# The first layer's mixer in another order: recurrence beside gate, k and v projections, heads between q tiles, last 16 tokens in blocks of 8 heads

## What is computed

```
proj = u @ w_in                      # gate 1024, xr 1024, q 1024, k 128, v 128 columns
xr = causal_dwconv(xr, conv_w, conv_b)                        # 4 taps
r = sigmoid(xr @ w_a + b_a); i = sigmoid(xr @ w_x + b_x)      # 8 blocks of 128
log_a = -8 * r * softplus(-lam)
h_t = a_t h_(t-1) + sqrt(1 - a_t^2) * i_t * xr_t
y_a = gelu(gate) * h
# 16 query heads of 64, 2 key heads; each token sees the last 128 tokens and the 16 first
s = q k^T / 8 - slope * distance      # masked
p = exp(s - mx) / (sum + exp(sink - mx)), mx = max(row maximum, sink)
y = concat([y_a, p v]) @ w_out
```

## Time and profile before

| | us |
|---|---|
| median of 3 runs | 3022.61 (3022.34 to 3024.46) |
| the profiled execution | 3022.86 |
| its span, first to last instruction | 3020.9 |
| TensorE busy | 2573.4 (85%) |
| VectorE busy | 783.7 (26%) |
| ScalarE busy | 538.1 (18%) |
| mean granted TensorE clock | 0.913 of full |

### The profile page before, as it was taken

One profiled execution on the slowest core, in us unless ns is written; L12 is line 12 of the kernel. 1 busy time (PEld: TensorE's weight loads), 2 busy tenths in 40 slices (PEclk: granted clock), 3 DMA queues, 4 the chain that ended last, 5 costly groups with the idle time before them and its releaser, 6 DMA issues. The chain is left out here.

```text
span 3020.9 us, 36570 instructions
## 1 busy us (share of the span) xinstructions
PE 2573.4 (85%) x15266; PEld 1670.1 (55%) x15266; DVE 783.7 (26%) x1880; ACT 538.1 (18%) x1351; POOL 15.7 (1%) x23
## 2 busy tenths in 40 slices
PE   3999976598998998878777749789899799998998
PEld 1785743387542443323232228547787688666876
DVE  1010156601211111111111122370441225623431
ACT  2110112301111221111111111331111111421110
POOL 0000000000000000000000000000000000100000
PEclk7999996899799999989988979759999899998999
DMA  6132330045369999999999953103233233122432
GB/s 257 70 112 97 112 143 25 6 153 209 149 267 421 420 420 421 420 421 420 421 421 421 421 237 126 56 1 112 98 137 121 104 140 140 56 76 92 140 117 78
DMA packets 88054, 608.36 MB, mean 201 GB/s; under 512 B 10512, under 2 KB 12944, under 8 KB 17200
## 3 DMA queue, kind: packets, MB, share of 16 engines
q1 hardware_dynamic: 84704, 599.82, 50.3%
q10 hardware_dynamic: 3088, 5.78, 0.5%
q0 software_dynamic: 96, 0.39, 0.0%
HBM read 604.91 MB, written 1.05 MB: 201 GB/s over the span
## 5 line engine op out<-in xcount | busy, mean ns | idle before, releaser
L482 PE MATMUL bank<-arena,ring 128*128 128x272 f32 (+2 forms) x3712 | 890.1, 403 | 37.4 <-DVEq L544 18.4
L482 PEld LDWEIGHTS bank<-arena,ring 128*128 128x128 f32 x3712 | 711.2, 192 | 212.2 <-issue 45.4
L2064 PE MATMUL bank<-arena 128*32 128x512 f32 x2304 | 286.0, 618 | 47.6 <-DMA arena<-in_w_e 47.6
L508 PE MATMUL bank<-arena,ring 128*128 128x272 f32 x1216 | 284.9, 398 | 6.6 <-DVE arena L1567 6.1
L508 PEld LDWEIGHTS bank<-arena,ring 128*128 128x128 f32 x1216 | 233.9, 193 | 57.5 <-DVE arena L1567 7.0
L1455 DVE TENSOR_TENSOR arena<-bank,arena 128x256 f32<-128x256 f32 x56 | 23.8, 425 | 844.1 <-PE bank L2043 844.1
L2064 PE MATMUL bank<-ring,arena 128*32 128x512 f32 x1280 | 166.2, 633 | 47.5 <-DMA ring<-in_w_e 47.4
L2064 PEld LDWEIGHTS bank<-arena 128*32 128x32 f32 x2304 | 64.4, 111 | 213.5 <-DMA arena<-in_w_e 105.9
L2081 PE MATMUL bank<-arena 128*32 128x256 f32 x1760 | 115.8, 404 | 44.5 <-DMA arena<-in_w_e 40.5
L1555 DVE SCALAR_TENSOR_TENSOR arena<-arena,par 128x272 f32<-128x272 f32 x296 | 148.6, 502 | 10.5
L2081 PE MATMUL bank<-ring,arena 128*32 128x256 f32 x1824 | 117.7, 406 | 29.4 <-DMA ring<-in_w_e 26.1
(11 more groups left out here) (361 smaller groups left out, 2009.5 us busy)
## 6 DMA issues: line engine op xcount, KB each, us to landing
arena<-in_w_e SPq DMA_DIRECT2D x224, 1024.0 KB, 25.9
ring<-in_w_e SPq DMA_DIRECT2D x160, 1024.0 KB, 26.2
ring<-in_w_up SPq DMA_DIRECT2D x44, 1024.0 KB, 4.8
ring<-in_w_l SPq DMA_DIRECT2D x37, 1024.0 KB, 4.8
ring<-in_w_ada SPq DMA_DIRECT2D x24, 1024.0 KB, 6.3
ring<-in_w_proj SPq DMA_DIRECT2D x24, 1024.0 KB, 4.8
ring<-in_w_down SPq DMA_DIRECT2D x32, 704.0 KB, 4.0
ring<-in_w_merge SPq DMA_DIRECT2D x16, 1024.0 KB, 4.8
```

The source lines that it names most:

```text
L482: mm = pe.matmul(o[:, 0:n], ring[:, s, k * 256 + c * P:k * 256 + (c + 1) * P], rhs(k), start=(k == 0), stop=(k == KT - 1))
L508: mm = pe.matmul(o[:, 0:n], ring[:, s, k * P:(k + 1) * P], rhs(part * kt + k), start=(part == 0 and k == 0), stop=(part == parts - 1 and k ...
L2064: mm = pe.matmul(bank[q * GROUP:(q + 1) * GROUP, 4 + g % 2, :], xe[:, (g // CHUNK) % 2, k, s:s + GROUP], w[:, q * 512:(q + 1) * 512], star ...
```

## The change

The columns of the input weights are laid out in another order: xr, gate, k and v, q.

The recurrence runs beside the projections. PE projects xr (4 units), one gate unit, the recurrence products of tiles 0 to 3, a gate unit, those of tiles 4 to 7, two gate units, then k and v. ACT copies the gate tiles as they are, and between them does sigmoids, tanh, exponentials and the square root. After the root it takes the 8 Gelus from SBUF, and then copies k and v. DVE does all 8 `lru_input`, waits for the root, does all 8 `lru_scan`, and only then begins on the heads.

The heads are worked on between the q tiles. PE does q tile j, the turn of head 2j-2, the values of pair j-2, the scores of head 2j, the turn of 2j-1 and the scores of 2j+1. The scores contract over all 128 rows: k lies in two copies `kz`, each with zeros in the half of the other key head, cleared by POOL. Only tokens 0 to 255 are done per head, in two strips side by side in one bank. Score strips and turned probabilities have four buffers instead of three and two. The banks are 0 to 2 for scores, 3 and 4 for turned probabilities and 5 for values.

The last 16 query tokens of 8 heads are laid side by side, 128 rows (`q_end`). Two such blocks (i = 16 and 17) go through the same steps with 272 columns. Slopes, sinks and penalties are laid out for them. The maximum with the sink and the change of sign are one instruction, with the sinks negated ahead.

Phases 10 and 11 are gone (later ones are renumbered), and the first products of the output projection wait for the single recurrence tiles and for the last pair of heads.

```diff
-    w0 = np.concatenate([w0[:, :2 * D], w0[:, 2 * D:3 * D][:, swap], w0[:, 3 * D:]], axis=1)
+    w0 = np.concatenate([w0[:, D:2 * D], w0[:, :D], w0[:, 3 * D:], w0[:, 2 * D:3 * D][:, swap]], axis=1)
...
# ScalarE
+            def gate_tiles(unit):
+                for n in (2 * unit, 2 * unit + 1):
+                    o, free = tile_out(act, at, n % 2 == 1)
+                    act.activation(ga[:, n, :], o[:, 0:L], ACT.Copy).then_inc(free, 1)
...
+            for unit in range(2):
+                gate_tiles(unit)
+                for n in range(4 * unit, 4 * unit + 4):
+                    lru_sigmoids(n)
             act.wait_ge(sem("lru_gate_read"), 8)
             act.wait_ge(sem("nlru_ready"), 1)
             for n in range(8):
                 act.activation(th[:, n, :], rg[:, n, :], ACT.Tanh, scale=lru2[:, n:n + 1]).then_inc(sem("lru_tanh"), 1)
+            gate_tiles(2)
             act.wait_ge(sem("lru_tanh"), 8)
             for n in range(8):
                 act.activation(rg[:, n, :], rg[:, n, :], ACT.Exp, scale=nlru[:, n:n + 1]).then_inc(sem("lru_decay"), 1)
+            gate_tiles(3)
+            act.wait_ge(sem("lru_ratio"), 8)
+            act.activation(th[:, :, :], th[:, :, :], ACT.Sqrt, scale=2.0).then_inc(sem("lru_root"), 1)
+            act.wait_ge(sem("bank_read0"), at.out // 2)
+            act.wait_ge(sem("bank_read1"), at.out // 2)
+            for n in range(8):
+                act.activation(ga[:, n, :], ga[:, n, :], ACT.Gelu_apprx_tanh).then_inc(sem("lru_gelu"), 1)
+            o, free = tile_out(act, at, False)
+            for s in range(2):
+                ins = act.activation(kz[64 * s:64 * s + 64, s, :], o[64 * s:64 * s + 64, 0:L], ACT.Copy)
+            ins.then_inc(free, 1)
...
+            for j in range(10):
+                if j >= 1:
+                    swa_exp(2 * j - 2)
+                    swa_exp(2 * j - 1)
+                if j < 8:
+                    o, free = tile_out(act, at, j % 2 == 1)
+                    act.activation(q0[:, j, 0:T], o[:, 0:T], ACT.Copy)
+                    act.activation(q_end[:, j, :], o[:, T:L], ACT.Copy).then_inc(free, 1)
+                if j >= 1:
+                    swa_copy(2 * j - 2)
+                if j >= 2:
+                    swa_result(j - 2)
+                if j >= 1:
+                    swa_copy(2 * j - 1)
...
# VectorE
+            for n in range(8):
+                lru_input(n)
+            dve.wait_ge(sem("lru_root"), 1)
+            dve.wait_ge(sem("lru_decay"), 8)
+            for n in range(8):
+                lru_scan(n)
...
+                dve.scalar_tensor_tensor(out=sc[:, b, 0:width], in0=cst("pen", 0 if i < HEADS2 else 3 * P, width),
+                                         scalar=cst("slope", i, 1), in1=bank[:, i % 3, 0:width],
+                                         op0=ALU.mult, op1=ALU.add).then_inc(sem("swa_masked"), 1)
+                dve.wait_ge(sem("swa_masked"), i + 1)
+                for t, (a, z) in enumerate(swa_spans(i)):
+                    ins = dve.reduce_max(smx[:, b, t:t + 1], sc[:, b, a:z], AX_X)
+                chain(ins)
+                n = len(swa_spans(i))
+                dve.tensor_scalar(snm[:, b, 0:n], smx[:, b, 0:n], -HD ** -0.5, nsink[:, i:i + 1], ALU.mult, ALU.min)\
+                   .then_inc(sem("swa_negmax"), 1)
...
+            for n in range(9):
+                swa_mask(2 * n)
+                swa_mask(2 * n + 1)
+                swa_probs(2 * n)
+                swa_probs(2 * n + 1)
...
# TensorE
-            project(pe, at, 12, ub_k, L)
+            project(pe, at, 4, ub_k, L)
+            for half in range(2):
+                project(pe, at, 1, ub_k, L)
+                for n in range(4 * half, 4 * half + 4):
+                    lru_gates(n)
+            project(pe, at, 2, ub_k, L)
...
+            def swa_scores(i):
+                if i >= 3:
+                    pe.wait_ge(sem("swa_masked"), i - 2)
+                b = i % 3
+                if i < HEADS2:
+                    j, s = i // 2, i % 2
+                    pe.wait_ge(sem(f"bank_read{(q_read + j) % NL}"), (q_read + j) // NL + 1)
+                    for t0 in (0, P):
+                        mm = pe.matmul(bank[:, b, t0:t0 + t0 + P], q0[:, j, t0:t0 + P], kz[:, s, 0:t0 + P], start=True, stop=True)
+                else:
+                    mm = pe.matmul(bank[:, b, 0:L], q_end[:, :, :].rearrange("p j t -> p (j t)"), kz[:, i - HEADS2, :], start=True, stop=True)
+                mm.then_inc(sem("swa_scores"), 1)
...
+            for j in range(10):
+                if j < 8:
+                    q_tile(j)
+                if j >= 1:
+                    swa_turn(2 * j - 2)
+                if j >= 2:
+                    swa_values(j - 2)
+                if j < 9:
+                    swa_scores(2 * j)
+                if j >= 1:
+                    swa_turn(2 * j - 1)
+                if j < 9:
+                    swa_scores(2 * j + 1)
+            swa_values(8)
+            project_deep(pe, at, 1, 2 * KT, lambda k: mix[:, k, :], L, first=first_mix)
```

More of the change, by code:

```diff
@@ L1094, in _ @@
[L1094 to L1106, removed]
@@ L1146, in _ @@
             conv_silu(CT - 1)
-            phase(act, 15)
+            phase(act, 13)
             def ssm_square(n):
@@ new lines, in swa_probs @@
+            def swa_probs(i):
+                b, n = i % 4, len(swa_spans(i))
+                dve.wait_ge(sem("swa_exp"), i + 1)
+                chain(dve.tensor_tensor(ssk[:, b, 0:n], ssk[:, b, 0:n], sden[:, b, 0:n], ALU.add))
+                chain(dve.reciprocal(ssk[:, b, 0:n], ssk[:, b, 0:n]))
+                for t, (a, z) in enumerate(swa_spans(i)):
+                    ins = dve.tensor_scalar(sc[:, b, a:z], sc[:, b, a:z], ssk[:, b, t:t + 1], None, ALU.mult)
+                ins.then_inc(sem("swa_probs"), 1)
@@ L1662, in _ @@
             post_norm("l0_post")
-            phase(dve, 12)
+            phase(dve, 10)
             ffn(0)
@@ L1712, in _ @@
                         read_x(i)
[L1713 removed]
+            phase(dve, 13)
             dve.wait_ge(sem("ssm_cb"), 1)
@@ L1768, in _ @@
             post_norm("l1_post")
-            phase(dve, 16)
+            phase(dve, 14)
             ffn(1)
@@ L1773, in _ @@
             post_norm("f1_post")
-            phase(dve, 17)
+            phase(dve, 15)
         @block.gpsimd
@@ L1784, in _ @@
             pool.memset(ys[:, :, :], 0.0).then_inc(sem("ys_cleared"), 1)
-            for n in range(6, 16):
+            for n in range(6, 10):
+                phase(pool, n)
+            pool.memset(kz[64:128, 0, :], 0.0)
+            pool.memset(kz[0:64, 1, :], 0.0).then_inc(sem("kz_cleared"), 1)
+            for n in range(10, 14):
                 phase(pool, n)
@@ L1789, in _ @@
                 pool.tensor_tensor(zs[:, n, :], zs[:, n, :], xb[:, n, :], ALU.mult).then_inc(sem("ssm_gated"), 1)
-            for n in range(16, LAST_PHASE + 1):
+            for n in range(14, LAST_PHASE + 1):
                 phase(pool, n)
@@ L2216, in _ @@
             at.unit += 1
-            pe.wait_ge(sem("lru_loaded"), 16)
-            for n in range(8):
-                pe.wait_ge(sem("xc_ready"), n + 1)
-                if n >= 2:
-                    pe.wait_ge(sem("lru_gate_read"), n - 1)
-                b = 2 * (n % 2)
-                pe.matmul(bank[:, b, 0:L], wlru[:, 0, n, :], xc[:, n, :], start=True, stop=True)
-                pe.matmul(bank[:, b + 1, 0:L], wlru[:, 1, n, :], xc[:, n, :], start=True, stop=True)\
-                  .then_inc(sem("lru_gates"), 1)
@@ new lines, in swa_turn @@
+            def swa_turn(i):
+                pe.wait_ge(sem("swa_probs"), i + 1)
+                if i >= 2:
+                    pe.wait_ge(sem("pt_ready"), i - 1)
+                p = sc[:, i % 4, :]
+                if i < HEADS2:
+                    for c in range(3):
+                        mm = pe.transpose(bank[:, 3 + i % 2, c * P:(c + 1) * P], p[:, c * P:(c + 1) * P], ident)
+                else:
+                    for c, (s0, m) in enumerate(TOK):
+                        mm = pe.transpose(bank[0:m, 3 + i % 2, c * P:(c + 1) * P], p[:, s0:s0 + m], ident)
+                mm.then_inc(sem("swa_turned"), 1)
@@ new lines, in swa_values @@
+            def swa_values(n):
+                pe.wait_ge(sem("pt_ready"), 2 * n + 2)
+                if n >= 1:
+                    pe.wait_ge(sem("swa_result"), n)
+                spans = ((0, T, 0, P), (P, T, T, P)) if n < 8 else ((0, P, 0, P), (0, P, P, P), (0, P, T, META))
+                for c, (a, z, at0, m) in enumerate(spans):
+                    for s in range(2):
+                        mm = pe.matmul(bank[64 * s:64 * s + 64, 5, a:z], v0[0:m, c, 64 * s:64 * s + 64],
+                                       pt[0:m, (2 * n + s) % 4, at0:at0 + z - a],
+                                       start=(c == 0), stop=(c == len(spans) - 1), skip_group_check=True)
+                mm.then_inc(sem("swa_pv"), 1)
@@ L2270, in _ @@
```

(4 more changed lines are left out.)

230 lines of the change are left out of this document (99 added, 131 removed).

## The result

| | before | after | both orders and the tail (last experiment) |
|---|---|---|---|
| median, us | 3023.53 | 2949.87 | 2928.24 |
| lowest to highest, us | 3022.34 to 3026.22 | 2947.8 to 2955.23 | 2925.79 to 2928.47 |
| ratio to before, with 95% interval | | 0.9757 (0.9745 to 0.9768) | 0.9679 (0.9666 to 0.9692) |
| span of the profiled run, us | 3020.9 | 2946.0 | 2925.0 |
| first projection product to first output product, us | 232.0 | 154.45 | (order differs) |

The change is worth 74 us by the medians; 2949.87 was measured and 2948 forecast. I call it the stretch. The row above it I call the mixer.

The account below looks back on a forecast made before the run. The heads' loop through TensorE, VectorE and ScalarE at the low clock was taken as the bound, projections by TensorE elsewhere. Cutting 232.0 us to 156.7 saves 75.3, giving 2948 us, range 2938 to 2972 (its own 2940 to 2962).

Parts of the forecast that it names:

- Projections and recurrence products: Before the heads: reordered tiles and recurrence pairs put TensorE at 54.4 us after two gate units, 78.4 after v.
- The stall at ScalarE's queue: Before the first q tile: TensorE waits 9.1 us for ScalarE's root, Gelus and k copies; bounds 3.6 to 14.
- Table loads: Before the Gelus on ScalarE: 1.3 us taken; the skill's added drain would make the sum 1.4 us larger.
- The rounds: One q tile with a pair of heads' transposes, scores and values: 6.95 us, TensorE longest, at full clock.
- The cover: Within each pair of heads: 4.6 us of TensorE work hides 4.0 us of VectorE and ScalarE, 0.6 to spare.
- The tail: After the last q tile: heads 14 and 15, then the two end blocks, 6.0 and 6.9 us, waits near 3.
- The output projection's clock: At the output projection's start: 0 to 2 us of gain if the clock stays up; 0 taken.
- The sum: First projection product to first output product: 232.0 before, 156.7 after, so 75.3 us saved.
- The rivals: For the whole kernel: low clock 3002 us, chance 0.11; no overlap 3049, 0.04; nothing moves 3015 to 3030, 0.02.
- The low clock: In the heads: TensorE stays at half clock, rounds of 13.9 us, kernel 3002 us; chance 0.11.
- The rounds overlapped as drawn: Against the rival that VectorE and ScalarE work follows the q tile: rounds 20.7 us, kernel 3049 us; chance 0.04.

Follow-up runs that it names:

- both orders and the tail (last experiment): Changed kernel with ScalarE's square root queued last, scans spread over the rounds, and early output-projection products filling TensorE's waits after the last q tile: 2928.24 us, ratio 0.9679.
- values head after head: Changed kernel with a pair's value products issued one head after the other instead of alternating between array halves: ratio 0.9756.
- both orders: Changed kernel with ScalarE's Gelus and k and v copies ahead of the square root, and scans spread over the first seven rounds: 2934.5 us, ratio 0.9701.
- the kernel without interleaving: Changed kernel with all eight q tiles projected before the first head instead of between the heads: ratio 0.9837.

## Why the prediction was right, step by step

*Projections and recurrence products.* Forecast 54.4 and 78.4 us from the first product. In the trace the later gate units start at 54.5 and the v tile ends at 78.4.

*The stall at ScalarE's queue.* Forecast 9.1, from 78.4 to 87.5; measured 8.6, to 87.0, with ScalarE's k copies as the releaser. The first mask was forecast at 95.5, and is there. The Gelus took 2.7 us instead of 3.4, and the root came 0.3 later. Three runs confirm the account behind it: removing the stall alone or VectorE's backlog alone moved nothing in the mixer.

*Table loads.* The load before the Gelus began at 1898.23 and the Gelus at 1899.52, 1.29 us, as in the earlier trace rows. The 2.66 us that the Trainium skill gives for a switch (ScalarE: Activation LUTs, What ACT_TABLE_LOAD costs) would, by an estimate from it, have put the first q tile 1.4 us later than it came.

*The rounds.* Forecast 6.95, measured 6.63. The term that was too large is the values: 1.3 for 768 columns one after the other at the projection's pace, 0.80 measured, because they run two at a time (above), which the prediction did not consider. Scores and turns came out about 0.1 larger each (1.41 and 0.75 against 1.3 and 0.66). Six rounds, 1.9 us. VectorE came to 4.5 us a round (26.8 over six rounds), not 5.0. The cover held: the probabilities of a pair's first head are ready 0.7 us before their turn (1920.79 and 1921.45).

*The tail.* Forecast 6.0 and 6.9, 12.9 together; measured 12.87, with waits of 2.9 and 2.3 us against "near 3".

*The output projection's clock.* I took 0 of a possible 2; it gained 1.8. The prediction said that it couldn't tell, and two other kernels (values head after head, both orders) began the output projection at 0.50: that it was gained here is luck.

*The sum.* Forecast 75.3 saved in the mixer, measured 77.55, and 79.3 in the stretch. The total came out at 73.7 by the medians, and at 74.9 by the profiled spans. For the latter the difference stands ahead of the change: the first projection product came at 1816.02 instead of 1812.13. Over the fourteen kernels here, which all do the same work up to there, it lies between 1810.8 and 1817.0. So 4 us of gain that the sum had missed (2.25 in the mixer, 1.8 in the output projection) were cancelled by scatter in the first block, and the agreement within 2 us is partly luck.

*The rivals.* The low clock did not stay through the heads. But the reasoning with which I set it aside was incomplete. I named the rows, the few columns and the waits for the old loop; the waits alone are refuted, the rows explain part, and the few columns were not tried. The rounds overlapped as drawn. In the kernel without interleaving they do not, and it stayed faster than before; that this is owed to its heads' clock (0.68 over its rounds, not 0.50) is argued, not shown.

## What to carry to other kernels

Put dense, independent work in the queue of the busiest engine at exactly the place where it waits for a chain of small steps: here seven q tiles, and then two half output tiles, vanished into waits of 3 us, and the clock was up besides. When removing a wait gains nothing, look at what is late next, and try the pair of edits before dropping either. Price a stage from profile rows at the clock that the new stage will have, and check the part ahead of the change before crediting a forecast, or an edit, with the last few microseconds.

## What the runs showed of the hardware that I had not expected

- TensorE can be almost without waits and stay at the low level: 91% busy over 84 us at 0.50 (88% over the whole loop of 104 us at 0.53), with 64-row scores and small strips among its products. The same loop with 128-row scores had 0.72 and took 11.7 us less.
- A change between products of 64 and of 128 rows costs at the full clock: 0.54 us a round with two such scores groups, seen as issue gaps of 0.33 us before the weight loads.
- Products with 64 columns of weights for the two halves of the array ran two at a time: 768 columns in 0.80 us, against 1.30 at the pace of 128 columns of weights. They did so even where the kernel issues all of one half's products before the other's.
- The clock in a tail with waits of 2 to 3.4 us is not steady from kernel to kernel: 0.87, 0.64 and 0.59 in windows of similar work. Between the first two, which differ only in the order of the values, it is worth 3.1 us in the mixer and 5.9 in the stretch (223.5 against 217.6).
